# Router logits in strips, idle products in TensorE's waits, and two signals given earlier

## What is computed

```python
x = x + gt_a * (y @ w_out)                          # the mixer's last product
u = modulate(rms_norm(x, norm_ffn_g), sh_f, sc_f)
scores = sigmoid(u @ router_w)                      # 256 x 16
# group-limited top 2 of 16 experts over scores + router_b -> combine (256 x 16)
for e in range(16):
    he = silu(u @ w_gate[e]) * (u @ w_up[e])
    out = out + combine[:, e:e+1] * (he @ w_down[e])
```

## Time and profile before

| | us |
|---|---|
| median of 3 runs | 604.17 |
| lowest, highest | 602.7, 604.27 |
| the profiled execution | 600.97 |
| its span, first to last instruction | 599.1 |
| PE busy in it | 577.4 (96%) |
| DVE, ACT busy | 306.9 (51%), 238.7 (40%) |

### The profile page before, as it was taken

The page is one execution under the profiler, slowest core; times in us unless marked ns, Lnnn a source line. Parts: engine busy times, 40 slices in busy tenths (PEclk is TensorE's granted clock), DMA queues, the critical chain, the costliest instruction groups (busy, mean ns, idle before and its releaser), DMA issues.

```text
span 599.1 us, 8462 instructions
## 1 busy us (share of the span) xinstructions
PE 577.4 (96%) x3563; PEld 423.3 (71%) x3563; DVE 306.9 (51%) x461; ACT 238.7 (40%) x330; POOL 9.0 (2%) x23
## 2 busy tenths in 40 slices
PE   3999999999999999999999999999999999999995
PEld 0789988999998888999999988533534444353432
DVE  0679976766568966677546683712212130221204
ACT  5617658444454545764683334701111020111113
POOL 3001000000000000000000000000000000000000
PEclk9999999999999999999999999999999999999998
DMA  8999664785859947636558989399999999999992
GB/s 309 387 332 323 212 206 140 282 287 209 287 209 341 328 170 279 220 107 237 198 217 318 416 341 357 154 378 423 421 419 422 423 421 419 422 421 422 421 382 78
DMA packets 51577, 184.78 MB, mean 308 GB/s; under 512 B 3649, under 2 KB 3761, under 8 KB 37713
## 3 DMA queue, kind: packets, MB, share of 16 engines
q1 hardware_dynamic: 50706, 183.53, 79.7%
q10 hardware_dynamic: 704, 0.58, 0.3%
q0 software_dynamic: 128, 0.11, 0.1%
HBM read 183.16 MB, written 1.05 MB: 307 GB/s over the span
## 4 chain that ended last, share of the span: by engine, by line
PE 90%; DVE 3%; ACT 3%; DMA 1%; issue 1%; SPq 0%; ACTq 0%; DVEq 0%
PE ps L1576 30%; PE ps L1788 18%; PE ps L1598 16%; PE ps L1800 8%; PE ps L1834 3%; PE ps L1776 2%; DMA first_ada<-in_ada_w_dram 1%; PE ps L1810 1%; PE ps L1683 1%; PE ps L1698 1%; PE ps L1662 1%; PE ps L1494 1%; PE ps L1827 1%; DVE lo L953 1%; PE ps L1587 1%
## 5 line engine op out<-in xcount | busy, mean ns | idle before, releaser
L953 DVE TENSOR_TENSOR lo<-raw,hi 128x2048 fp32r<-128x2048 f32 (+1 forms) x51 | 114.2, 2248 | 41.2 <-ACT hi L613 40.8
L1576 PE MATMUL ps<-u_hi,hi 128*128 128x256 f32 x416 | 120.3, 289 | 0.7 <-DVE lo L953 0.7
L1576 PE MATMUL ps<-u_lo,hi 128*128 128x256 f32 x416 | 117.9, 283 | 0.0
L1576 PE MATMUL ps<-u_hi,lo 128*128 128x256 f32 x416 | 117.9, 283 | 0.0
L1788 PE MATMUL ps<-ring,xe_t 128*64 128x512 f32 x512 | 111.7, 593 | 0.0
L613 ACT CAST hi<-raw 128x2048 fp32r<-128x2048 f32 x50 | 94.9, 1908 | 36.0 <-PE ps L1576 25.5
L1788 PEld LDWEIGHTS ps<-ring,xe_t 128*64 128x64 f32 x512 | 36.5, 137 | 71.7 <-issue 71.4
L1576 PEld LDWEIGHTS ps<-u_hi,hi 128*128 128x128 f32 x416 | 79.8, 192 | 2.1 <-DVE lo L953 1.1
L1576 PEld LDWEIGHTS ps<-u_lo,hi 128*128 128x128 f32 x416 | 79.9, 192 | 0.2
L1576 PEld LDWEIGHTS ps<-u_hi,lo 128*128 128x128 f32 x416 | 79.9, 192 | 0.0
L1800 PE MATMUL ps<-ring,he_t 128*64 128x512 f32 x224 | 49.6, 596 | 0.0
(11 more groups left out here) (334 smaller groups left out, 837.0 us busy)
## 6 DMA issues: line engine op xcount, KB each, us to landing
raw<-in_w_in_dram SPq DMA_DIRECT2D x41, 1024.0 KB, 5.2
ring<-in_w_gate_e_dram SPq DMA_DIRECT2D x32, 1024.0 KB, 17.4
ring<-in_w_up_e_dram SPq DMA_DIRECT2D x32, 1024.0 KB, 16.0
ring<-in_w_down_e_dram SPq DMA_DIRECT2D x28, 1024.0 KB, 16.0
raw<-in_ada_w_dram SPq DMA_DIRECT2D x16, 1024.0 KB, 5.3
first_ada<-in_ada_w_dram SPq DMA_DIRECT2D x16, 512.0 KB, 11.8
raw<-in_w_branch_m_dram SPq DMA_DIRECT2D x4, 1024.0 KB, 5.5
raw<-in_w_out_dram SPq DMA_DIRECT2D x4, 1024.0 KB, 6.1
```

What stands on the lines that cost most here:

```text
L953: ins = V.tensor_tensor(lo[b % RING][:, tiles, :], src[:, tiles, :], hi[b % RING][:, tiles, :].bitcast(F32), ALU.subtract)
L1576: ins = mm(dst, w[:, k, cols], x[:, k0 + k, :], start=(first and c % 2 == 0 and k == 0 and n == 0), stop=(end and k == KB - 1 and n == 2), ...
```

## The change

1. `mod_p` becomes two events, `mod_p0` and `mod_p1`, and each half of `ffn_col` waits for its own.
2. The logits of channels 0 to 511 come from four products instead of eight: `rw_scaled[:, n:n+2]` (32 columns, of which the last 16 belong to the next chunk and are not used) is stationary, the turned rows of both tiles (256 columns) move, and chunk n writes to partitions 32n to 32n+31 of bank 5. ACT copies the 128 x 256 result to `strips` (in the place of `x_res_t[0]`'s first chunk), and two products with `pick_e`, a 128 x 16 matrix of zeros and ones, add up the four strips into the logits' bank, ahead of `logits(0)`. `pick_e` is one reduction of `ident` on DVE at the second `ffn_col` half.
3. Idle products whose results are not read (`keep_busy`): 8 of 256 columns (fp32r) ahead of the fourth block's first wait, 1 (fp32r) ahead of the wait for tile 1's rows, and 4 (float32) instead of 1 ahead of the wait for "picked". `start_sums(0, 0)` moves ahead of the wait for the last logits.
4. The first tile's one-hot has a signal of its own, and the first four gather products run tile by tile.

```diff
-            pe += ["wo_t0", "wo_t1_0", "x1_turn1_t0", "logits0", "x1_turn1_t1", "logits1", "bcast3", "rank_sums"]
-            act += ["x1_ss1_t0", "x1_turned1_t0", "x1_sqrt0", "x1_ss1_t1_0", "x1_ss1_t1_1", "x1_turned1_t1", "x1_sqrt1", "scores",
+            pe += ["wo_t0", "logit_strips", "wo_t1_0", "x1_turn1_t0", "logits0", "x1_turn1_t1", "logits1", "bcast3", "rank_sums"]
+            act += ["strips", "x1_ss1_t0", "x1_turned1_t0", "x1_sqrt0", "x1_ss1_t1_0", "x1_ss1_t1_1", "x1_turned1_t1", "x1_sqrt1", "scores",
...
                     for m in range(2):
-                        ins = nc.scalar.copy(dealt(mod_p[:, m, :]), nearby(mod[:, 1 + m, :]))
-                    event(ins, "mod_p")
+                        event(nc.scalar.copy(dealt(mod_p[:, m, :]), nearby(mod[:, 1 + m, :])), f"mod_p{m}")
...
+            after(act, "logit_strips")
+            event(nc.scalar.copy(strips, ps[5][:, 0:T]), "strips")
             x1_square(0, slice(NB, D), 10, "x1_ss1_t0", "x1_1_t0", "x1_ss0")
...
+                    V.tensor_reduce(pick_e[:], ident[:].rearrange("p (i j) -> p j i", i=4)[:, 0:NE, :], AX_X, ALU.add)
...
-            ins.then_inc(onehot_ready, 1)
+                ins.then_inc(onehot_ready if t else onehot_first, 1)
...
+            def keep_busy(bank, count, left, right):
+
+                for _ in range(count):
+                    mm(ps[bank][:, 0:T], left, right, start=True, stop=True)
+
-            def logits(t, h):
+            def logits(t):
...
+                if s == EARLY:
+                    keep_busy(6, 8, u_hi[:, 0, 0:P], u_hi[:, 0, :])
...
                             after(pe, "x1_turned0", "logit_shift")
-                            logits(0, 0)
-                            logits(1, 0)
+                            for n in range(KB):
+                                strip_ins = mm(ps[5][32 * n:32 * n + 32, 0:T], rw_scaled[:, n:n + 2, :].rearrange("p a e -> p (a e)"),
+                                               x_res_t[0][:, n, :], start=True, stop=True, skip_group_check=True)
+                            event(strip_ins, "logit_strips")
...
-                    after(pe, "mod_p", "a_turned3")
                     m = FFN_COL_AT.index(s)
+                    after(pe, f"mod_p{m}", "a_turned3")
...
+            after(pe, "strips")
+            for t in range(TT):
+                mm(ps[4][:, t * NE:(t + 1) * NE], strips[:, t * P:(t + 1) * P], pick_e[:], start=(t == 0), stop=False,
+                   skip_group_check=True)
             after(pe, "x1_turned1_t0")
-            event(logits(0, 1), "logits0")
+            event(logits(0), "logits0")
+            keep_busy(1, 1, y_hi[:, 0, 0:P], y_hi[:, 0, :])
...
+            start_sums(0, 0)
             after(pe, "x1_copied1_t1", "x1_turned1_t1")
-            event(logits(1, 1), "logits1")
+            event(logits(1), "logits1")
...
             evacuated(pe, 26)
-            start_sums(0, 0)
-            for _ in range(1):
-                mm(ps[3][:, 0:T], ident[:], mod[:, 0, 0:T], start=True, stop=True)
+            keep_busy(3, 4, ident[:], mod[:, 0, 0:T])
             after(pe, "picked")
...
             after(pe, "xg_hi0_0", "xg_hi1_0")
-            pe.wait_ge(onehot_ready, 1)
-            gather_part(0, 4 * SLOTS, 4, (0,))
+            for t in range(TT):
+                pe.wait_ge(onehot_ready if t else onehot_first, 1)
+                for kk in range(2):
+                    mm(ps[4][:, kk * T:(kk + 1) * T], xg_hi[:, t, kk * P:(kk + 1) * P], onehot[:, t, :],
+                       start=(kk == 0 and t == 0), stop=False, skip_group_check=True)
```

More of the change, by code:

```diff
@@ L246, in build @@
         gm = small("gm", [P, 12, TT, MH])
+        strips = x_res_t[0][:, 0, :]
         neg_row = h_m[0:MH, 0, 0:T]
@@ L252, in build @@
         ffn_g = small("ffn_g", [P, 2, KB])
+        pick_e = small("pick_e", [P, NE])
         logit_shift = small("logit_shift", [P, NE])
@@ L281, in build @@
         xe_early = sem("xe_early")
+        onehot_first = sem("onehot_first")
         onehot_ready, slots_turned, gathered, xe_act, xe_dve, scat_ready, scattered = (sem(n) for n in (
@@ L348, in plan @@
                 if s == M_TURN_AT[1]:
-                    act += ["ha_hi", "mod_p"]; dve.append("ha_lo")
+                    act += ["ha_hi", "mod_p0", "mod_p1"]; dve.append("ha_lo")
                 if s == FFN_COL_AT[1]:
@@ L1525, in _ @@
                 mm(ps[1][:, 0:T], ident[:], first_ada[0][:, 0, 0, 0:T], start=True, stop=True)
-            def logits(t, h):
+            def keep_busy(bank, count, left, right):
+                for _ in range(count):
+                    mm(ps[bank][:, 0:T], left, right, start=True, stop=True)
+            def logits(t):
                 for k in range(KB):
-                    ins = mm(ps[4][:, t * NE:(t + 1) * NE], x_res_t[h][:, k, t * P:(t + 1) * P], rw_scaled[:, KB * h + k, :],
-                             start=(t == 0 and h == 0 and k == 0), stop=(h == 1 and k == KB - 1), skip_group_check=True)
+                    ins = mm(ps[4][:, t * NE:(t + 1) * NE], x_res_t[1][:, k, t * P:(t + 1) * P], rw_scaled[:, KB + k, :],
+                             start=False, stop=(k == KB - 1), skip_group_check=True)
                 return ins
@@ L1744, in _ @@
             event(ins, "x1_turn1_t1")
-            after(pe, "x1_copied1_t1", "x1_turned1_t1")
-            event(logits(1, 1), "logits1")
             def start_sums(t, h):
                 mm(ps[2 * t + h][:], ident[:], x_res[:, t, h * NB:(h + 1) * NB], start=True, stop=False, skip_group_check=True)
+            start_sums(0, 0)
+            after(pe, "x1_copied1_t1", "x1_turned1_t1")
+            event(logits(1), "logits1")
             for n in range(2):
```

## The result

| | before | after |
|---|---|---|
| median of the timed executions, us | 604.16 (602.7 to 604.27, n = 4) | 598.75 (598.39 to 599.14, n = 4) |
| the profiled execution, us | 600.97 | 599.14 |
| its span, us | 599.1 | 597.3 |

The ratio is 0.9924, 95% interval 0.9899 to 0.9948: 0.76% faster, 5.4 us by the medians. The two profiled executions differ by only 1.8. That gap, 5.4 against 1.8, is what the experiments had to explain; the forecast of 602.3 had subtracted a gain of this size (1.9) from the timed median.

What follows compares the result with a forecast made beforehand. PE was taken to bound the kernel, holding 90% of the chain of waits; gains of 1.0 + 0.9 = 1.9 us off the timed median of 604.17 gave 602.3. The range was 599.9 to 603.8.

Steps and rivals of the forecast that it cites:

- 1. mod_p: At ffn_col: signalling mod_p per half lets PE start the first half earlier; gain 1.0 us, ends 0 and 1.05.
- 2. Eight idle products at the fourth block: Before the fourth block: eight products take 1.0 us in a wait of 0.94, about 1.1 by issue; cost 0.
- 3. Strips: Route stretch, logits of channels 0 to 511: 0.6 us instead of 1.69; gain 1.1, other end a loss of 0.1.
- 4. Fillers in the chain: Route stretch: pick products 0.1 us late, moved start_sums cost 0, idle products before rank sums 0.1; 0.9 of 1.1 left.
- 5. The one-hot's signal: First gather products: two can start 0.4 us earlier, but low-part products still wait for DVE; gain 0, at most 0.1.
- The first rival: Timed runs fall to the low clock in the quiet route stretch; idle products win back 2.4 us more: 599.9; chance 0.2.
- The third rival: Idle products at the low clock cost double ahead of needed products: 3.2 us against 1.9 gained, 605.5; chance 0.06.
- The second rival: Strips without overlap or with drains: route gives -0.5 to 0.3 us instead of 0.9; 603.2, no measurable change; chance 0.2.

## Why the prediction was wrong

The step that failed is the last line of the sum: "The median of the three timed runs is 604.17, above the profiled one by 3.2; less 1.9 that is 602.3". It took those 3.2 us for a constant of the timing, which the changed kernel would have too. The runs showed falls of PE's clock in their place, which the change removes. The measured 598.75 lies 3.6 under the forecast and 1.2 under the range's low end.

The 5.4 us between the medians can be laid out by the later executions. 604.16 is 1.5 above the median of before over 63 executions, 602.69. This median is 1.4 above the 601.26 of those at 0.997, which is what the falls cost the median execution. The path is 2.1 shorter. That leaves 0.4, which is less than the scatter of the first block's start and is not explained. So the size of the miss is in part chance: with 602.69 as the base, the same sum gives 600.8. The 1.5 of the first four executions are likely falls too, by their times; whether there were more of them by chance or by the chip is open.

The terms of the path, by the steps:

1. mod_p: forecast 1.0, measured 1.05 to 1.1 (311.32 stands one spacing behind 311.20). What was missed is that the same wait is followed by a low clock in a part of the executions, 1.5 us each, right on block products. Two traces show that, both of kernels that keep this wait; two more traces keep it without a fall, and none of the ten with the wait gone has one. I had priced the wait, not what it does to the next 3 us. Of the four edits tried alone on the kernel before, the split is the only one that moves the timed median: 2.5 in its group.
2. Eight idle products at the fourth block: 0 in the path, measured 0 (1.10 us in a wait of 1.10). Right. What they do for the clock is shown by the traces together: four of the six profiled executions with this wait unfilled fall there, none of the eight with it filled. For the changed kernel by itself it is not: without them two of six executions are at 0.995 (none of ten with them), and its one trace has no fall.
3. Strips: forecast 0.6 for the eight instructions, measured 0.57 (365.95 to 366.52); gain forecast 1.1, measured 1.04. From the last 512-column product before them (365.63) to tile 1's first product it is 0.89 now, and was 1.93:

```profile
366.54 0.39 PE L1598 MATMUL ps<-lo,y_hi 128*128 128x512 f32 x1
366.77 1.85 PE L1530 MATMUL ps<-rw_scaled,x_res_t 128*128 128x16 f32 x16
...
368.47 0.37 PE L1587 MATMUL ps<-hi,y_hi 128*128 128x256 f32 x1
```

The share for column tiles in the Trainium skill's "TensorE: Matmul & The Clock Gate", "Part 3: Packing small matmuls", would give, as an estimate, 0.7 with the forecast's 0.15 for entry and exit. The trace is nearer to four strips side by side. The drain at a change of tiling mode that the Trainium skill's "TensorEngine Tiling (Array Packing)", "Key Properties", states is small here: the first strip follows the product before it by 0.32, where the logits of before followed by 0.23, and 0.57 is 0.13 over the 0.44 of streaming alone; 0.22 in all at the most.
4. Fillers in the chain: forecast 0.1 late for the turns, 0.1 for the picks. The turns went to 371.44 from 373.29, 2.1 earlier by the corrected start, and PE reached the rank products without a wait: both together cost less than 0.1. The 0.9 that the forecast left of the strips is 1.0 in the path of the kernel without them.
5. The one-hot's signal: 0, measured 0.

The whole path: forecast 1.9, measured 2.1. So the forecast was right for an execution without a fall (600.97 to 599.1; measured 599.14), and wrong for the median.

The first rival, a clock drop that the profile missed, had the cause right at a chance of 0.2, and 599.9. Its price of 2.4 was that of one place, the route. The traces have three places, at 44 to 49, 314 to 318 and 373 to 380 us, and 34 of 63 executions of before lie at 0.992 or less. These traces are of kernels that keep some of the waits of before; the only profiled execution of before itself has no fall, so its own three places are inferred. Its counterargument was void: one profiled execution at a full clock says nothing about the others, while three timed ones all 1.7 to 3.3 us above it did say something, and I gave that too little weight.

The third rival's mechanism, idle products at half clock standing ahead of needed ones, did not come in the changed kernel, but the start with 18 idle products shows that it is real (3.36 for 1.97, first block 0.9 late). The second rival is out by the strips' 0.57.

That the route's fillers and the moved seed hold the clock up is seen in the two kernels that differ in them alone: without them 5 of 12 executions are at 0.990 to 0.993, and the profile has the fall of 6.8 us; with them none of 6 is below 0.995. Six are few, but of the nine traces with the moved seed and fillers none falls in the route, of the five without them two do, and in all 45 executions of the seven kernels that have the moved seed and the split signal none is below 0.995. The moved seed with one idle product on each side is enough (none of six below 0.996). Which of the two matters, and how often each of the three places falls by itself in before, was not measured: an execution's mean clock doesn't name the place.

## What to carry to other kernels

When timed executions lie over the profiled one by more than they scatter about each other, look for clock falls before building on the median: sort executions by mean granted clock, and profile one of the low ones. Price a PE wait twice, by its length and by a fall behind it. In all three places here sparse products (one to 16 moving columns, turns) stood beside the wait; that they matter was not tested by itself. An edit that shortens the work between two waits can give its gain back to the clock, as the strips alone seem to have done; real work moved into the wait (the accumulator's seed) fills it for nothing.

## What the runs showed of the hardware

- A wait of 0.89 to 0.94 us of PE by the modelled ends, about 1.1 by issue, with sparse products beside it, was followed by 3.3 to 3.4 us at about half the clock (0.50 and 0.53; 1.2 of 2.4 GHz). In the route the longest wait beside the fall was 0.59, and the low stretch was 3.3 us in one trace and 6.8 in another. The profiled execution of before has the same waits and no fall, and 1.3 us of waiting before the picks went without one in the profile, with all six executions at 0.996 or more.
- How many falls an execution has differs from one to the next: 23 of 63 of before were at 0.997, five at 0.987.
- One such fall cost 0.9 us at the fourth block, 1.5 at ffn_col and 1.0 (2.6 for the long one) in the route, by the path in the traces.
- The granted clock prints 1.00 from 0 to 14 us although product rows there are at the low level (eight instructions in 1.94, later 1.06): before the first change is recorded, only the products tell.
